# Attention in steps of four key tiles, its loads after the projections, and seven smaller moves in a fused decoder layer

## What is computed

```python
h = rms_norm(x, norm);  proj = h @ w_in                      # 2048 -> 14k columns
# A: mLSTM, 4 heads of 256, causal conv of 4 taps on q/k, exponential gates
hm = rms_norm(mlstm_chunkwise(q, k, v, ig, lf)) * sigmoid(m_o) * silu(m_z)
# B: latent attention, 8 heads, 128 plain + 64 rotary dimensions, causal
q_all = rms_norm(a_cq) @ w_uq; kv = rms_norm(a_ckv) @ w_ukv  # latents of 512
ha = causal_softmax_attention([q_nope, rope(q)], [k_nope, rope(k_r)], v) * silu(a_z)
# C: 4 heads of 256 over 256 memory tokens
hc = softmax(c_q @ mk.T / 16) @ mv * silu(c_z)
merged = sig(g_m) * (hm @ w_m) + sig(g_a) * (ha @ w_a) + sig(g_c) * (hc @ w_c)
out = rms_norm(x + merged @ w_out, final_norm)
```

## Time and profile before

| | us |
|---|---|
| median of 3 runs | 2751.95 |
| lowest, highest | 2750.35, 2952.0 |
| the profiled execution | 2748.97 |
| its span on the slowest core (core 1) | 2747.7 |
| spans of the eight cores | 2732.5 to 2747.7 |
| busy: PE, DVE, ACT, POOL | 2693.6, 1059.3, 892.9, 617.0 |

### The profile page before, as it was taken

How to read it: one execution, slowest core, us unless ns; L and a number is a source line. 1 busy time by engine, 2 the same in 40 slices (tenths; PEclk the granted TensorE clock), 3 DMA queues, 4 the chain that set the end, 5 groups by cost and what they waited for, 6 DMA issues and landing times.

```text
span 2747.7 us, 41837 instructions; the slowest of 8 cores (2732.5 to 2747.7 us)
## 1 busy us (share of the span) xinstructions
PE 2693.6 (98%) x14037; PEld 1300.4 (47%) x14037; DVE 1059.3 (39%) x1788; ACT 892.9 (32%) x1741; POOL 617.0 (22%) x924
## 2 busy tenths in 40 slices
PE   7999899999999999999999999999999999999998
PEld 3544344564446644454555444444444444444444
DVE  6645377548576556244434311111111111111433
ACT  5532356436565454254544211111111111110212
POOL 0003100100210121277760122222222222221000
PEclk9999999999999999999999999999999999999999
DMA  9657724532544324556645744445475544447562
GB/s 252 130 131 159 193 62 108 117 98 55 105 104 108 78 41 86 96 141 155 166 107 147 170 77 76 78 74 79 77 165 92 95 75 77 76 78 131 193 206 87
DMA packets 142211, 312.38 MB, mean 114 GB/s; under 512 B 14833, under 2 KB 73009, under 8 KB 134961
## 3 DMA queue, kind: packets, MB, share of 16 engines
q0 software_dynamic: 42048, 134.27, 30.6%
q1 hardware_dynamic: 95634, 162.32, 18.9%
q10 hardware_dynamic: 4320, 13.11, 1.5%
HBM read 371.22 MB, written 72.68 MB: 162 GB/s over the span
## 4 chain that ended last, share of the span: by engine, by line
PE 92%; DMA 5%; ACT 1%; DVE 1%; issue 1%; POOL 1%; SPq 0%; ACTq 0%; POOLq 0%; DVEq 0%
PE bk L290 91%; DMA xt<-x 1%; DMA xo<-x 1%; DMA QRT<-ob 1%; DMA cz<-CZ 0%; DMA HMT<-hm 0%; PE bk L514 0%; SPq L135 0%; DMA QNT<-ob 0%; DMA mb<-BH 0%; PE bk L535 0%; PE bk L1188 0%; PE bk L1234 0%; DVE ro L303 0%; PE bk L1338 0%
## 5 line engine op out<-in xcount | busy, mean ns | idle before, releaser
L290 PE MATMUL bk<-hT,wg 128*128 128x512 bf16 x3072 | 682.3, 380 | 0.0
L290 PE MATMUL bk<-w,hT 128*128 128x512 bf16 (+1 forms) x3072 | 598.3, 345 | 7.5 <-DMA w<-wA 2.9
L290 PE MATMUL bk<-hT,w 128*128 128x512 bf16 x2112 | 489.6, 380 | 0.0
L290 PEld LDWEIGHTS bk<-hT,wg 128*128 128x128 bf16 x3072 | 300.5, 98 | 361.5 <-issue 1.6
L290 PEld LDWEIGHTS bk<-w,hT 128*128 128x128 bf16 x3072 | 296.3, 98 | 251.8 <-issue 16.2
L294 ACT ACTIVATE sh<-bk 128x512 f32<-128x512 f32 x184 | 109.8, 597 | 850.1 <-PE bk L290 850.1
L290 PE MATMUL bk<-hb,wb 128*128 128x512 bf16 x1536 | 346.7, 379 | 0.0
L290 PEld LDWEIGHTS bk<-hT,w 128*128 128x128 bf16 x2112 | 204.9, 98 | 228.8 <-issue 4.7
L310 DVE SCALAR_TENSOR_TENSOR tm<-sh,bk 128x512 f32<-128x512 f32 x124 | 85.3, 688 | 559.2 <-PE bk L290 559.2
L290 PEld LDWEIGHTS bk<-hb,wb 128*128 128x128 bf16 x1536 | 150.1, 98 | 181.1
L303 DVE TENSOR_TENSOR den<-den,Pa 128x512 f32<-128x512 f32 (+3 forms) x288 | 186.4, 647 | 103.4 <-ACT Pa L294 75.1
(11 more groups left out here) (180 smaller groups left out, 2433.1 us busy)
## 6 DMA issues: line engine op xcount, KB each, us to landing
wg<-wGB POOLq DMA_DIRECT2D x96, 512.0 KB, 5.3
w<-wA POOLq DMA_DIRECT2D x48, 516.0 KB, 9.2
wb<-wGB POOLq DMA_DIRECT2D x96, 256.0 KB, 4.1
xt<-x SPq DMA_DIRECT2D x16, 1024.0 KB, 13.3
xo<-x SPq DMA_DIRECT2D x16, 1024.0 KB, 6.8
out<-xo SPq DMA_DIRECT2D x15, 1024.0 KB, 7.4
wo<-wOUT POOLq DMA_DIRECT2D x4, 2048.0 KB, 17.5
w<-wA POOLq DMA_DIRECT2D x16, 500.0 KB, 12.2
```

What stands on the lines that cost most here:

```text
L290: fw.op("pe", lambda e: e.matmul(bk[o] if not isinstance(o, bass.AP) else o, lhsT=lhsT, rhs=rhs, start=start, stop=stop), reads=reads, wri ...
```

## The change

Nothing of the mathematics changes. The parts:

1. Front: for tiles 1 to 4 xt * gx is made first (DVE, into xg), then scaled by rstd, half on DVE, half on ACT; write(i) stands ahead of step(x=i + 1). Of the four waiting latents none is transposed at i == 5, two at i == 6, two at i == 7.
2. ob has two resources per tile (n=2), and uq stores each half when it is full.
3. mla_gen does nothing until MLA; then come its allocations and all loads.
4. Scores in groups of four key tiles over all heads; the scores of a group are issued before the P.V matmuls of the group before. Pa has 8 tiles, den 3. The normalization's exp and log come with its matmuls. Ratio 0.345 for 0.38, and other yields.
5. mLSTM: the gate set-up starts at V1, the rest at ML, which is set at tile 1 of oz3; mg is loaded at the start of a chunk; HMT is stored from ACT's queue.
6. c_gen yields 8 + 1 for 4 + 4 before its first scores; d_gen loads wb after each of the first gate units.
7. End: xo before gfin and wo3; three of the last four blocks are scaled on DVE.

```diff
@@ p0_gen
-                    if i < 5:
+                    if 0 < i < 5:
+                        for hf in range(2):
+                            c = slice(hf * 1024, hf * 1024 + 1024)
+                            tt("dve", xg[:, c], xt[:, c], gx[:, c], ALU.mult, [xt.r, gx.r], [xg.rs[hf]])
+                        ts("dve", xb[:, 0:1024], xg[:, 0:1024], rs_, None, ALU.mult, None, [xg.rs[0], r_], [xb.rs[0]])
+                        act(xb[:, 1024:2048], xg[:, 1024:2048], AF.Copy, [xg.rs[1], r_], [xb.rs[1]], scale=rs_)
+                    elif i == 0:
...
             for i in range(5):
+                write(i)
                 step(x=i + 1)
-                write(i)
...
-                if i == 5:
-                    pend.extend(old[2:])
-                    del old[2:]
+                keep = 0 if i == 5 else 2
+                pend.extend(old[keep:])
+                del old[keep:]
@@ p1_gen
-            ob = Ring(tiles("ob", 6, [128, S], BF16))
+            ob = Ring(tiles("ob", 6, [128, S], BF16, n=2))
...
+            def half(o, tb):
+                return ([], [o.rs[tb // 2]]) if tb % 2 else ([o.rs[tb // 2]], [])
...
-            marks.add("MLA0")
...
-                    for ci in (2, 0, 1):
+                    for ci in ((2, 0, 1) if pr or tb else (0, 1, 2)):
...
-                for ci in range(2):
-                    hh = 2 * pr + ci
-                    fw.dma("sp", QNT_d[hh * 128:(hh + 1) * 128, :], o3[ci][:], reads=[o3[ci].r], accs=[dr("QNT", hh)])
-                fw.dma("sp", QRT_d[pr * 128:(pr + 1) * 128, :], o3[2][:], reads=[o3[2].r], accs=[dr("QRT", pr)])
-                if pr == 0:
-                    marks.add("UQ0")
+                    if tb % 2:
+                        c = slice(tb * 512 - 512, tb * 512 + 512)
+                        for ci in range(2):
+                            hh = 2 * pr + ci
+                            fw.dma("sp", QNT_d[hh * 128:(hh + 1) * 128, c], o3[ci][:, c], reads=[o3[ci].rs[tb // 2]], accs=[dr("QNT", hh)])
+                        fw.dma("sp", QRT_d[pr * 128:(pr + 1) * 128, c], o3[2][:, c], reads=[o3[2].rs[tb // 2]], accs=[dr("QRT", pr)])
@@ mla_gen
+            yield ("need", "MLA")
             kr = mem.alloc("kr", [128, S], BF16, top=True)
...
-            yield ("need", "UQ0")
             loads_qk(0)
-            yield ("need", "MLA")
...
+            def emit_S(h, qb, kq):
...
+                for k in range(4 * kq, 4 * kq + 4):
+                    n = (4 * qb + 4 - max(k, 4 * qb)) * 128
+                    its.append((k, n, slice(4 * qb * 128 + 512 - n, 4 * qb * 128 + 512), slice(k * 128, (k + 1) * 128), SBk.next()))
+                for k, n, qc, kc_, (bs, r_bs) in its:
+                    mm(bs, r_bs, (slice(None), slice(0, n)), kn[:, kc_], qn[:, qc], True, False, [kn.r, qn.r])
+                for k, n, qc, kc_, (bs, r_bs) in its:
+                    hf = slice(64 * (k % 2), 64 * (k % 2) + 64)
+                    mm(bs, r_bs, (slice(None), slice(0, n)), kr[hf, kc_], qr[hf, qc], False, kq < qb, [kr.r, qr.r])
...
+            nxt = emit_S(*groups[0])
+            yield 7 * MM
+            for gi, (h, qb, kq) in enumerate(groups):
+                cur_ = nxt
+                if gi + 1 < len(groups):
+                    nxt = emit_S(*groups[gi + 1])
+                    yield 6 * MM
...
+                for k, p, n in cur_:
+                    mm(po, r_po, (slice(None), slice(512 - n, 512)), vx[:, k, :], p[:, 0:n], k == 0, k == 4 * qb + 3, [vx.r, p.r])
                     tick()
+                    yield MM * n / 512
@@ mlstm_gen
-            yield ("need", "ML")
...
+            yield ("need", "ML")
             hm2 = tiles("hm", 1, [128, 8, 256], BF16, top=True)
...
-                loads_g(c + 2)
...
-                    fw.dma("sp", HMT_d[cp // 4, :, cp % 4, :], hm2[0][:].rearrange("p a b -> p (a b)"), reads=[hm2[0].r], accs=[dr("HMT", cp // 4)])
+                    fw.dma("act", HMT_d[cp // 4, :, cp % 4, :], hm2[0][:].rearrange("p a b -> p (a b)"), reads=[hm2[0].r], accs=[dr("HMT", cp // 4)])
...
+                if c > 0:
+                    loads_g(c + 1)
@@ c_gen
-            yield 4.0
+            yield 8.0
             P["mtail"]()
...
-            yield 4.0
+            yield 1.0
@@ d_gen
-            for _ in range(4):
-                bload()
...
+                bload()
...
-                    if n4 % 2:
+                    if n4:
...
             for t in range(6):
                 xload(t)
+                if t == 3:
+                    fw.dma("sp", gfin[:], gf_d, writes=[gfin.r])
+            for r in cur[2].rs:
+                fw.wait_res("pool", r)
+            wo_load(3, wo3)
@@ sides
-        sides = [(mla_gen, "MLA0", 0.38), (mlstm_gen, "ML", 0.34), (c_gen, "CZ0", 0.7)]
+        sides = [(mla_gen, "MLA", 0.345), (mlstm_gen, "V1", 0.34), (c_gen, "CZ0", 0.7)]
```

More of the change, by code:

```diff
@@ L687, in p1_gen, with part @@
             cqnT, ckvnT = P["cqnT"], P["ckvnT"]
-            ob = Ring(tiles("ob", 6, [128, S], BF16))
-            def part(o, c, bk, r_bk, first):
-                evac_copy(o[:, c], bk[:, 0:512], [r_bk], [o.r] if first else [], [] if first else [o.r])
+            ob = Ring(tiles("ob", 6, [128, S], BF16, n=2))
+            def part(o, tb, bk, r_bk):
+                evac_copy(o[:, tb * 512:(tb + 1) * 512], bk[:, 0:512], [r_bk], *half(o, tb))
+            def half(o, tb):
+                return ([], [o.rs[tb // 2]]) if tb % 2 else ([o.rs[tb // 2]], [])
             def rotate(o, tb, bk, r_bk):
@@ L698, in rotate @@
                 tt("dve", t2[64:128, :], bk[0:64, 0:512], sinT[0:64, cols], ALU.mult, [r_bk, sinT.rs[tb]], [], [t2.r])
-                tt("pool", o[:, cols], t1[:], t2[:], ALU.add, [t1.r, t2.r], [o.r] if tb == 0 else [], [o.r] if tb else [])
+                tt("pool", o[:, cols], t1[:], t2[:], ALU.add, [t1.r, t2.r], *half(o, tb))
             def part_v(o, u, bk, r_bk):
@@ L886, in v_block @@
             if jv == 1:
+                marks.add("V1")
                 mem.release(bif)
@@ L958, in mla_gen @@
             kns = tiles("kn", 2, [128, S], BF16, top=True)
-            vxs = tiles("vx", 1, [128, 16, 128], BF16, top=True)
+            vxs = tiles("vx", 2, [128, 16, 128], BF16, top=True)
             for lo, src in ((0, 0), (32, 64), (64, 32), (96, 96)):
@@ L1029, in finish @@
                 later(4, f2)
-                later(5, f3)
+                later(4, f3)
                 later(7, f4)
@@ L1034, in mla_gen @@
             loads_az(0)
[L1035 removed]
+            groups = [(h, qb, kq) for h in range(8) for qb in range(4) for kq in range(qb + 1)]
+            accd = {}
+            def emit_S(h, qb, kq):
                 i = h % 2
[L1037 to L1079 removed]
@@ new lines, in emit_S @@
+                qn, qr, kn = qns[i], qrs[i], kns[i]
+                if kq == 0:
+                    accd[h, qb] = accs_.next()
+                acc = accd[h, qb]
+                its = []
+                for k in range(4 * kq, 4 * kq + 4):
[3 more added lines that the diff above has]
+                    mm(bs, r_bs, (slice(None), slice(0, n)), kn[:, kc_], qn[:, qc], True, False, [kn.r, qn.r])
@@ new lines, in emit_S @@
+                for k, n, qc, kc_, (bs, r_bs) in its:
+                    hf = slice(64 * (k % 2), 64 * (k % 2) + 64)
+                    mm(bs, r_bs, (slice(None), slice(0, n)), kr[hf, kc_], qr[hf, qc], False, kq < qb, [kr.r, qr.r])
+                if kq == qb:
+                    for k, n, qc, kc_, (bs, r_bs) in its:
+                        mm(bs, r_bs, (slice(None), slice(0, 128)), identb[:], mneg[:], False, True, [RC, mneg.r])
+                res = []
+                for k, n, qc, kc_, (bs, r_bs) in its:
+                    p = Ps.next()
+                    act(p[:, 0:n], bs[:, 0:n], AF.Exp, [r_bs], [p.r], scale=SC)
+                    if k == 0:
+                        copy("dve", acc[:], p[:], [p.r], [acc.r])
+                    else:
+                        o = 512 - n
+                        tt("dve", acc[:, o:512], acc[:, o:512], p[:, 0:n], ALU.add, [acc.r, p.r], [acc.r])
+                    res.append((k, p, n))
@@ L1104, in mlstm_gen @@
             act(tmpg[:], tmpg[:], AF.Ln, [tmpg.r], [tmpg.r], bias=1.0)
+            yield 1.5
             bk, r_bk = misc.next()
@@ L1111, in mlstm_gen @@
             stt(At[:], GIv, -LN64, Bt[:], ALU.add, ALU.subtract, [r_gif, Bt.r], [At.r])
-            yield 1.0
+            yield 1.5
             tt("dve", tmpg[:], Gt[:], At[:], ALU.add, [Gt.r, At.r], [tmpg.r])
```

73 lines of the change are left out of this document (19 added, 54 removed).

## The result

The changed kernel is slower: it took 2842.0 to 2846.5 us in four executions, where I had forecast 2729 (2722 to 2733) and had put 0.01 on anything above 2807. The ratio to the kernel before is 1.0339, 95% interval [1.0319, 1.036]. The profiled execution took 2841.96 us, its span is 2840.7 (core 2) where before had 2747.7.

A forecast was written before the change was run, and what follows sets the result against it. TensorE was taken as the limit, idle 2.5 of 705.9 us in attention. Terms +1.0 -10.6 +14.1 -16.0 -2.2 +4.0 -8.2 -3.6 -1.4 gave -22.9: 2724.8 from the span 2747.7, 2729 in medians, range 2722 to 2733.

The forecast's parts named there:

- the burst of exps and adds (+4.0): Attention, v0 and v1: four exps and four adds at once outlast short dense units; 0.2 us for some 20 groups, +4.0.
- Rival 4: Attention: bursts of adds on DVE hold dense banks, making it slower than before; at 0.5 us a group 2765; chance 0.08.
- The fours' own gain (-16.0): Attention scores: entering and leaving the 64-row shape costs 0.20 us, paid once per four key tiles instead of two; -16.0.
- Rival 2: Attention scores: the entering and leaving cost stays with each couple of rotary matmuls; 2737; chance 0.10.
- Projection (-10.6): Rotary query projection: without early attention loads and with half stores, the whole 10.6 us lost to idle and low clock returns.
- Rival 5: Query projection: the change does not free the ring of ob tiles, stores still queue; +5, 2734; chance 0.05.
- Loads of head 0 (+14.1): First attention scores: later loads beside a weight load stall TensorE 11.5 us, plus 2.6 of low clock; +14.1.
- Rival 1: First attention scores: head 0's loads come in time, no stall or low clock; 2715; chance 0.22.
- mLSTM (-8.2): mLSTM: early gate set-up saves 1.0, HMT stored from ACT's queue removes hm's wait of 6.2, clock 1.0; -8.2.
- rival 3: mLSTM: the HMT store is no earlier on ACT's queue; 2729 + 7.2 = 2736; chance 0.08.
- Cross-attention (-3.6): Cross-attention: wb loads moved after gate units and more side yield remove rdc waits and low clock; -3.6, bounds -4.1 and 0.
- Front (+1.0): Kernel's start: tile 6 wait -0.7, later transposes +0.45, low clock +1.3; +1.0, bounds -1 and +3; early product worth 0.

The follow-up runs named there:

- the last runs in fours: Changed kernel with all repairs to loads, normalization, v units and mLSTM start, sums at tick 3: 2739.5 us; the same with attention's ratio 0.32 for 0.345: 2742.5.

## Why the prediction was wrong, step by step

- **Attention: the failing step.** I had -14.2 for the fours, and alone they brought +78.7. I costed the burst of exps and adds (+4.0), and of the yields and the normalization's new ticks only where attention ends (0). That the cast, the sums and the log are counted in P.V matmuls, and that after the edit scores and adds of the next group are queued ahead of them, I did not follow; a wait of TensorE on this chain stood nowhere in my sum. The chain measured 56.8 us of waits. With GIF's 16.8 and the clock at 0.97 over 825.8 us (some 0.03 x 825.8 = 25) it closes: the gap is 93 us; 56.8 and the 12.8 of GIF beyond my 4.0 leave 23 for the clock. I had written that stalls in places which had none would prove me wrong; so it was.
- **Rival 4** named the right engine and burst, and its GIF waits in v0 and v1 were the sign to look for. Its place was as I said, where 1.74 us units don't cover four adds. Only the size was off: 16.8 us, or 0.8 for each of some 20 groups where I took 0.2. By itself it is under the point from which it would have decided (0.34 x 80 = 27). A rival "the normalization is waited for" was missing, and what spoke for it stood in the diff: yields of 2.5 MM between ticks became 1, and a group of scores is issued ahead.
- **The fours' own gain (-16.0):** right, by the start times in the kernel after; the last runs in fours agree. Rival 2 is out: the second couple starts without a pause. The Trainium skill's rule that a change of tiling mode drains the array (TensorEngine Tiling, Tiling Modes, Key Properties) agrees: 0.10 in, 0.10 out, once a group. The waits for Pa (-2.2) went too.
- **Projection (-10.6):** right on the slowest core, 52.0 to 41.4 us, no wait on ob. But 52.0 was the worst of eight: from its first to its last matmul the projection took 43.6 to 51.6 us by core before, and 41.2 or 41.3 on every core after, as it did in all three other kernels with the late loads. With early loads it took 41.2 to 48.3 us by core in the four kernels with attention in twos, where stores go in halves, and 41.5 to 46.8 in the fours put into the kernel before, where they don't. So what frees the ring is the order of the loads on SP. That the stores in halves add to it is not shown: no kernel has late loads and whole stores. Rival 5 is out.
- **Loads of head 0 (+14.1):** the stall is there but was mis-sized: 17.8 us for 11.5, just past its bound of 17. The stretch ahead of the first scores grew from 15.5 to 33.5 us, and low clock follows it. kr, qr, kn and qn were issued by 290.4 and qn landed at 311.8; I had the weight load done near 301 and 5 us for the rest. What it costs the whole, 14.1 by the spans, equals the forecast by luck: it is some 20 us at this place, less what the late loads save in the projection and what e waited less. Rival 1 is out.
- **mLSTM (-8.2):** hm's wait is gone. The store is issued 1.07 us after the start of the copy and lands in 3.8 us (median), so rival 3 is out. The rule on issuing engines (the Trainium skill, DMA: Bandwidth & Descriptors, Issuing engines are not separate DMA queues) would have kept the wait, but it is about starting a DMA; here the store stood in SP's order for 11.2 us, and that went. But the part's other half, the start at tile 1, cost 8 us with attention in twos, where I had put it at nothing: I had asked what is queued behind BH's round trip, not what mb meets on the way. With the fours, putting the start back gave no gain that can be told (2774.2 to 2772.2), so for the changed kernel itself this price isn't shown.
- **Cross-attention (-3.6):** not seen. The waits on rdc fell, and one on ho took their place: its ring of two waits for the store into HCT, 3.96 and 2.82 us on ACT in the kernel after.
- **Front (+1.0):** -0.5 by the start of the projection (237.4 to 236.9), inside my bounds but with the other sign. The wait of the transposes on c went from 3.1 to 0.4 us; the waits on xb stayed at 5.5, and 1.7 on ACT's sj is new.
- **End (-1.4):** -1.0 came by the stretch from the first hb matmul to the last of all (1189.1 to 1188.1 us), and the wait on xo is gone. From the add into the last block to the end of its scaling it took 3.6 us for 4.2, the forecast 0.6, but the span ended no earlier behind the last matmul: 7.4 us before, 7.7 after.

## What to carry to other kernels

When work is put off by a count of other instructions, a change of what lies between them changes its time. List for each deferred step what will be ahead of it in every queue after the change, and what its result's bank or buffer holds up. Issuing a step earlier in one chain puts it ahead of the others in every in-order queue, so the operation that a short chain waits for is best put down before the next batch. And set the gain beside the hand-overs: 0.2 us for each of 80 groups was on offer, and 56.8 us of waits, 1.8 for each of 32 query blocks, came.

Read a stage on all cores before taking its slowest core's loss as the gain.

## What the runs showed of the hardware

- Behind waits of 1.81 and 0.92 us the granted clock was 0.50 (434.4 to 436.0), and three matmuls took 1.16 us, where they took 0.81 at 449.22; behind a wait of 4.41 us they took 1.46. The mean granted clock in attention was 0.97, and 1.00 in the kernel before.
- The log on ACT has a table load of 1.28 us ahead of it; at 452.41 this did not start before its activation's buffer was free, so the two waits came one after the other instead of beside each other. The Trainium skill (ScalarE activation tables: per-element evaluation and per-set limits, What a function is on this engine) puts two functions in different sets 1283 ns apart; the row agrees.
- The loads of mb, 256 KB each, took 16.1 us (median of three) to land beside a weight load and 8.6 without one.
